# Plain down steps of a Strassen FFN: two output tiles side by side in two banks

## What is computed

```python
def swiglu(x, wg, wu, wd):
    return (jax.nn.silu(x @ wg) * (x @ wu)) @ wd

for layer in range(DEPTH):                       # DEPTH = 2
    x = x + 0.5 * swiglu(rmsnorm(x, norm_g[layer, 0]), ffn_w_gate[layer, 0], ffn_w_up[layer, 0], ffn_w_down[layer, 0])
    x = x + mixer(rmsnorm(x, norm_g[layer, 1]))  # layer 0: pooling || Hyena; layer 1: 2-D neighbourhood attention
    x = x + 0.5 * swiglu(rmsnorm(x, norm_g[layer, 2]), ffn_w_gate[layer, 1], ffn_w_up[layer, 1], ffn_w_down[layer, 1])
```

## Time and profile before

| | |
|---|---|
| median of 3 runs | 1871.65 us (1871.01 to 1871.67) |
| profiled execution | 1871.8 us, span 1870.0 us |
| TensorE (PE) | 1858.8 us busy, 99% |
| weight loads (PEld) | 1562.0 us busy, 84% |
| VectorE (DVE) | 1221.2 us busy, 65% |
| ScalarE (ACT) | 781.5 us busy, 42% |
| GpSimd (POOL) | 241.0 us busy, 13% |

### The profile page before, as it was taken

How to read it: one execution, slowest core, us unless ns; L and a number is a source line. 1 busy time by engine, 2 the same in 40 slices (tenths; PEclk the granted TensorE clock), 3 DMA queues, 4 the chain that set the end, 5 groups by cost and what they waited for, 6 DMA issues and landing times.

```text
span 1870.0 us, 24853 instructions
## 1 busy us (share of the span) xinstructions
PE 1858.8 (99%) x9540; PEld 1562.0 (84%) x9540; DVE 1221.2 (65%) x1866; ACT 781.5 (42%) x1280; POOL 241.0 (13%) x183
## 2 busy tenths in 40 slices
PE   8999999999999999999999999999999999999999
PEld 6888988877688988988889898888777788989887
DVE  7686865575566857755667685556676666858643
ACT  5343433443243433434434343345566443433331
POOL 0310400003201203100031130001111002104000
PEclk9999999999999999999999999999999999999999
DMA  5244232232032332322223232322222232322321
GB/s 185 74 141 118 91 113 91 87 128 90 22 114 101 107 108 89 113 92 90 92 76 127 92 107 99 109 67 87 72 72 84 68 113 73 125 96 91 113 91 68
DMA packets 65905, 181.23 MB, mean 97 GB/s; under 512 B 13608, under 2 KB 26569, under 8 KB 65802
## 3 DMA queue, kind: packets, MB, share of 16 engines
q1 hardware_dynamic: 52192, 169.89, 26.4%
q10 hardware_dynamic: 13610, 9.93, 1.9%
HBM read 177.70 MB, written 3.93 MB: 97 GB/s over the span
## 4 chain that ended last, share of the span: by engine, by line
PE 98%; DVE 1%; DMA 0%; ACT 0%; issue 0%; SPq 0%; ACTq 0%; DVEq 0%
PE bank L1306 25%; PE bank L1307 25%; PE bank L1308 25%; PE bank L1258 6%; PE bank L1261 5%; PE bank L1262 5%; PE bank L1426 1%; PE bank L1593 1%; PE bank L1577 1%; PE bank L1439 1%; PE bank L1417 1%; PE bank L1447 0%; PE bank L1565 0%; DMA x<-in_x_tokens 0%; PE bank L1406 0%; PE bank L1369 0%
## 5 line engine op out<-in xcount | busy, mean ns | idle before, releaser
L1306 PE MATMUL bank<-xh,whr 128*128 128x512 f32 x1408 | 550.4, 391 | 3.9 <-DVE xl L868 2.3
L1307 PE MATMUL bank<-xl,whr 128*128 128x512 f32 x1408 | 547.9, 389 | 0.0
L1308 PE MATMUL bank<-xh,wlr 128*128 128x512 f32 x1408 | 547.9, 389 | 0.0
L466 ACT ACTIVATE whr<-rest 128x512 fp32r<-128x512 f32 (+1 forms) x414 | 254.4, 616 | 500.6 <-PE bank L1308 498.7
L475 DVE TENSOR_TENSOR wlr<-rest,whr 128x512 fp32r<-128x512 f32 (+1 forms) x414 | 303.6, 735 | 160.3 <-ACT whr L466 156.3
L1307 PE MATMUL bank<-hsl,whr 128*128 128x256 f32 (+1 forms) x1040 | 321.5, 309 | 0.0
L1308 PE MATMUL bank<-hsh,wlr 128*128 128x256 f32 (+1 forms) x1040 | 321.5, 309 | 0.0
L1306 PE MATMUL bank<-hsh,whr 128*128 128x256 f32 (+1 forms) x1040 | 321.4, 309 | 0.0
L1306 PEld LDWEIGHTS bank<-xh,whr 128*128 128x128 f32 x1408 | 264.3, 188 | 62.6 <-DVE xl L868 2.8
L1308 PEld LDWEIGHTS bank<-xh,wlr 128*128 128x128 f32 x1408 | 264.3, 188 | 55.1
L1307 PEld LDWEIGHTS bank<-xl,whr 128*128 128x128 f32 x1408 | 264.4, 188 | 54.9 <-issue 1.0
(11 more groups left out here) (184 smaller groups left out, 1997.7 us busy)
## 6 DMA issues: line engine op xcount, KB each, us to landing
rest<-in_ffn_w_up SPq DMA_DIRECT2D x62, 512.0 KB, 4.5
rest<-in_ffn_w_gate SPq DMA_DIRECT2D x61, 512.0 KB, 3.6
rest<-in_ffn_w_down SPq DMA_DIRECT2D x42, 512.0 KB, 4.3
raw_area<-in_ffn_w_gate SPq DMA_DIRECT2D x26, 512.0 KB, 3.6
raw_area<-in_ffn_w_up SPq DMA_DIRECT2D x26, 512.0 KB, 4.5
raw_area<-in_w_qkv SPq DMA_DIRECT2D x24, 512.0 KB, 3.3
raw_area<-in_ffn_w_down SPq DMA_DIRECT2D x22, 512.0 KB, 4.3
raw_area<-in_w_in_ab SPq DMA_DIRECT2D x16, 512.0 KB, 3.3
```

The costliest lines, as they stand in the source:

```text
L466: act.activation(whr[:, at:at + st.kb, :].rearrange("p k c -> p (k c)"), weights(st, buf)[:, 0, :], ACT.Copy).then_inc(high, 1)
L1306: pe.matmul(out, whr[:, at, :], hi, start=start, stop=False, skip_group_check=onto)
L1307: pe.matmul(out, whr[:, at, :], lo, start=False, stop=False, skip_group_check=onto)
L1308: return pe.matmul(out, wlr[:, at, :], hi, start=False, stop=stop, skip_group_check=onto)
```

## The change

The two output tiles of a plain step are worked on side by side. Blocks are taken in pairs: the first pair holds the weights of both output tiles for the first half of the hidden tiles, the second pair those for the second half. Within a pair the matmuls go in turn between the two banks: for each hidden tile high x high into bank one, high x high into bank two, then high x low into both, then low x high into both. Which raw buffer a block is split from follows (`block_buf`). Both banks are full only at the end of the step, so both evictions come at blocks 2 and 3, and the residual work of both tiles stands in the next step (or behind the run).

```diff
+        def block_buf(st, n):
+
+            return {"up": B_A11 + n, "plain": B_A11 + 2 * (n % 2) + n // 2, "down": PRODUCTS[n].buf}[st.kind]
...
-                half = n // 2 if st.kind != "down" else int(PRODUCTS[n].buf == B_A22)
+                half = n // 2 if st.kind == "up" else n % 2 if st.kind == "plain" else int(PRODUCTS[n].buf == B_A22)
...
                         if n == 0 and prev and prev.kind == "plain":
+                            residual_of(prev, 0)
                             residual_of(prev, 1)
...
-                            if n == 2 and st.kind == "plain":
-                                residual_of(st, 0)
...
+                residual_of(ph.steps[-1], 0)
                 residual_of(ph.steps[-1], 1)
...
                     if st.kind == "plain":
-                        if n % 2:
-                            d = st.d[n // 2]
-                            add(st, n, x[:, d, :], bank[st.bank[n // 2]][:, :], 1)
+                        if n >= 2:
+                            add(st, n, x[:, st.d[n % 2], :], bank[st.bank[n % 2]][:, :], 1)
                         return
...
                         if n < 2 and prev and prev.kind == "plain" and FFN_NEXT[prev.ffn] is not None:
-                            (add_squares_of if n else part_low)(FFN_NEXT[prev.ffn], prev.d[1])
+                            for d in prev.d:
+                                (add_squares_of if n else part_low)(FFN_NEXT[prev.ffn], d)
...
-                            if n > 1 and st.kind == "plain" and FFN_NEXT[st.ffn] is not None:
-                                (part_low if n == 2 else add_squares_of)(FFN_NEXT[st.ffn], st.d[0])
...
                 if ph.next:
                     last = ph.steps[-1]
-                    part_low(FFN_NEXT[last.ffn], last.d[1])
+                    for d in last.d:
+                        part_low(FFN_NEXT[last.ffn], d)
                     split_low(dve, ph.next, 0, 1)
-                    add_squares_of(FFN_NEXT[last.ffn], last.d[1])
+                    for d in last.d:
+                        add_squares_of(FFN_NEXT[last.ffn], d)
...
-                def plain_block(st, n):
+                def plain_blocks(st, n):
+
+                    pe.wait_ge(low, ph.unit(st, n + 1) + 1 + LOW_CREDIT)
+                    place = slice(n, n + 2)
                     for k in range(st.half):
-                        if st.pair == 0 and n < 2 and k in (0, st.half - 1):
+                        if st.pair == 0 and k in (0, st.half - 1):
                             pe.wait_ge(hl_done, st.split0 + 2 * st.half - (0 if n and k else 1))
...
+                        hi = hsh[:, k, place, :].rearrange("p s t -> p (s t)")
+                        lo = hsl[:, k, place, :].rearrange("p s t -> p (s t)")
+                        first, final = n == 0 and k == 0, n == 2 and k == st.half - 1
+                        at = [(st.block0 + n + d) % 4 * (KD // 2) + k for d in range(2)]
+                        for part, (w, h) in enumerate(((whr, hi), (whr, lo), (wlr, hi))):
+                            for d in range(2):
+                                last = pe.matmul(bank[st.bank[d]][:, :], w[:, at[d], :], h, start=first and part == 0,
+                                                 stop=final and part == 2)
+                                if part == 2 and k == st.half - 1:
+                                    last.then_inc(unit_done, 1)
```

More of the change, by code:

```diff
@@ L464, in block_high @@
             at = v % 4 * (KD // 2)
-            buf = B_A11 + n if st.kind != "down" else PRODUCTS[n].buf
+            buf = block_buf(st, n)
             act.activation(whr[:, at:at + st.kb, :].rearrange("p k c -> p (k c)"), weights(st, buf)[:, 0, :],
@@ L1362, in ffn_run @@
                         pe.wait_ge(low, ph.unit(st, n) + 1 + LOW_CREDIT)
-                        {"up": up_block, "down": down_block, "plain": plain_block}[st.kind](st, n)
+                        if st.kind == "plain":
+                            if n % 2 == 0:
+                                plain_blocks(st, n)
+                        else:
+                            (up_block if st.kind == "up" else down_block)(st, n)
             def norm_mean(norm):
```

## The result

| | before | changed |
|---|---|---|
| median | 1871.47 us (20 runs, 1869.80 to 1872.83) | 1875.3 us (20 runs, 1873.18 to 1875.82) |
| ratio | | 1.0019, 95% interval 1.0013 to 1.0026 |
| span of the profiled execution | 1870.0 us | 1873.6 us |

The forecast was 1874.4 us, +2.8. The median is 1875.3 us, +3.8, and the profiled executions differ by +3.6.

A forecast was written before the change was run, and what follows sets the result against it. TensorE, busy 1858.8 of 1870.0 us, was taken to bound the kernel at 226.7 ns per matmul. Terms 0 + 1.66 + 0.49 + 0.62 = +2.77 us gave 1874.4 us, range 1871.0 to 1877.0.

The forecast's parts named there:

- The order of the matmuls: Plain steps, 768 matmuls: alternating banks changes nothing, 0 us; bounds 10.2 us less to 79 us more.
- the 8.4 us: Plain steps: lower sum by the Trainium skill's 215.8 ns per matmul, 768 x 10.9 ns, if alternation reaches it.
- The ring inside the stage: Split weights in plain stages: blocks come free in pairs each 5.44 us, 2.8 us of slack, so 0.
- Starts of w_in and qkv: First unit of each waits for tile d0's eviction: 0.83 us each, +1.66 us for two; bounds 0.66 and 1.0 each.
- What is covered by that stall: Starts of w_in and qkv: last xl, next low split and last add of squares all ready before needed, no cost.
- The border from FFN 1 to FFN 2: At 897.98 us: the mean's matmul waits for later adds of squares, +0.49 us; bounds 0 and 1.0.
- The end: Kernel's end: four output issues on one queue, the last 0.62 us later; bounds 0.4 and 1.0.
- (a): Plain steps: sustained alternation removes the fixed 13.3 ns per matmul, 10.2 us less, 1864.2 us; chance 0.10.
- (b): Clock falls once more (1876.1 us) or in each of four plain stages (1881.2 us), so slower; chance 0.16.
- (c): Border stalls hidden by faster signals, or the w_o clock drop vanishes (-1.7 us): about 1871.7 to 1872.9; chance 0.08.

The follow-up runs named there:

- order run: Changed kernel, but the two blocks of a pair worked one after the other, 12 matmuls into the first bank, then 12 into the second: 1873.23 us, ratio 1.0008.
- eviction run: Changed kernel, with the first unit of w_in and of qkv allowed to start with two evictions open instead of one: 1873.64 us, ratio 1.0015.

## Why the prediction was right, and where its terms were off

**The order of the matmuls (0).** Right. The bank change in the earlier trace rows was the nearest row and told the truth; the order run shows it directly. The Trainium skill ("TensorE: Matmul & The Clock Gate", section "Back-to-back issue gap") calls N/2.4 + 2.5 ns the gap of an isolated matmul, and gives about 131 ns a matmul for a stream of weight load and matmul pairs at 512 columns; I had named only the first. The trace agrees with neither: the mean spacing is 226.7 ns or more in every plain stage of every run, so the 8.4 us are not there.

**The ring inside the stage (0).** Right, no distance above 228 ns in any plain stage of the changed kernel.

**Starts of w_in and qkv (+0.83 each).** The mechanism was right, the term too small: +1.04 and +1.05. I took the restart from the earlier trace rows as 0.06 us; in the changed kernel it was 0.26, and the spacing took another 0.12 us to settle where I had allowed 0.11.

**What is covered by that stall (0).** This step failed in qkv. I put the last add's end at T + 6.4, needed at T + 6.95. With T = 1253.38 it ended at 1260.92, T + 7.54, and cost 0.59 us. I had priced the adds by their undisturbed 0.68 us and looked only at what stands ahead of them on VectorE, not at what GpSimd does at that time. The change moved the last add from T + 3.77 to T + 5.69, and there the mask (T + 5.43 to T + 7.00) was in work. I had also priced the late DMA issues on ScalarE at nothing because their data are "needed 20 us on". GpSimd takes them up as soon as they land, so that reason was wrong, but they are not the cause: in the order run they were not late, and the add ended at the same place. In w_in, which has no mask, the cover held.

**The border from FFN 1 to FFN 2 (+0.49).** Right in kind, too large: +0.20. The adds ended at T + 6.10 (904.89 - 898.79), not T + 6.44. ScalarE's row of two splits, xh, square, xh, square takes 0.10 us less a piece than its durations add up to, because each starts that much before the one ahead ends, and I had allowed 0.05 to 0.08.

**The end (+0.62).** Too small: +0.81. Four issues on one queue do not keep the pace of two; the third and fourth took 0.47 and 0.48 us with 0.50 between their starts, where I had 0.34 and 0.46 with 0.37 between them.

**Sum.** Predicted 2.77; the six sections give 3.69. With +0.09 in w_o, -0.28 at the kernel's start, which varies, and 0.05 elsewhere, this is the 3.55 us between the spans. The direction and the four places were right for the reasons given, and the sum was 0.9 us short: 0.4 at the two starts, 0.6 for the adds, 0.2 at the end, less 0.3 that the border was priced too high. That last error brought the total nearer by luck.

**Rivals.** (a) is refuted by the spacing. (b) is refuted: the clock is 1.00 in the plain stages, and no wait at a border was followed by a fall. (c) has two halves. That the stalls are hidden is refuted: in the eviction run they moved to the next wait instead. The fall in w_o does vanish in some executions, of the kernel before too, so it is no effect of the change; without it w_o is 1.4 to 1.6 us shorter, where I had 1.7. That the medians still compare well rests on most runs of both kernels having it: the mean clock is under 1.000 in 16 of the changed kernel's 20 runs and in 21 of the 26 of the kernel before named above. The range of (c) was also added up from two bases: from 1874.4 it is 1871.6 to 1872.7, not 1871.7 to 1872.9.

## What to carry to other kernels

When every instruction of the bounding engine keeps its price, reordering can change the time only at the seams. List each wait that counts "all but the last n" of something, and ask whether the last n are still the same ones. Stalls in series share their time: mend them together or the second takes what the first gives. And an instruction off the critical path that is moved later may begin beside another engine's: look at what is in work at its new place before it is given its old duration. Where an effect is tenths of a microsecond, cut the traces at the same instructions and compare the pieces; the medians here also carry a fall of the clock that comes and goes.

## What the runs showed of the hardware

- A matmul stream with a weight load each runs at 120 ns for 256 columns and 226.7 ns for 512, whatever the bank order (both widths in float32r; at 512 columns also in bfloat16). 64 rows instead of 128 give 226 or 227 ns in 181 of 191 distances; 64 weight columns instead of 128 make it 230.0 ns.
- A VectorE add of two SBUF tiles (128x512, float32) that began while a GpSimd tensor_tensor of 1.56 us was in work took 1.85 us instead of 0.69 and ended 0.55 us after it; an add that was already in work kept 0.68 us, and the GpSimd instruction took up to 1.97.
- A wait of about 2 us of TensorE was followed by 3.4 us at half clock in 5 of 12 profiled executions, worth 1.4 to 1.6 us each time; the waits of 0.4 to 1.4 us at the borders were followed by none.
- Output DMA issues on one queue start 0.37 us apart for the first two and 0.50 for the next two.
